# Input weights kept and reloaded by chunks of 128 columns through four slots; token chunks that hold both blocks; turned values written back into the output tile

## The chip, the cores and the metric

The kernel runs on one core of one Trainium2 chip. The metric is the device time of one execution in microseconds (us), lower is better. All data are float32.

## What is computed

One layer of an encoder trunk on x of 1024 tokens by 1024 channels: a projection of the normed input into 3592 columns, two groups of heads that mix the tokens, an output projection, and a feed-forward part that gathers expert rows.

```python
def hybrid_layer(x, ...):
    h = rms_norm(x, norm1_w)
    proj = jnp.einsum('bsd,dc->bsc', h, w_in)
    ...   # q, k, v of the attention heads; q, k, v, gate, a, b of the delta net
    o_sb = rms_norm(stick_breaking_attention(sq, sk, sv), ...)
    qkv = jax.nn.silu(causal_depthwise_conv(gdn_qkv, gdn_conv_w))
    ...
    o_gdn = rms_norm(gated_delta_net(gq, gk, gv, log_decay, write), gdn_out_norm_w) * gate
    x = x + jnp.einsum('bsc,cd->bsd', jnp.concatenate([o_sb, o_gdn], -1), w_out)
    x = x + peer_ffn(rms_norm(x, norm2_w), peer_w_q, ...)
    return x

def peer_ffn(hn, ...):   # for each token 8 heads x 16 experts out of 16384
    u = u_table[eb]                                   # 128 rows of 4 KB a token
    act = gelu(einsum('thkd,td->thk', u, xb)) * gb
    vv = v_table[eb]                                  # 128 more
    return einsum('thk,thkd->td', act, vv)
```

## The kernel before, in words

The eight blocks of 128 tokens are worked through one after the other. Two loads dominate: for each block, 128 gathers of `peer_u` rows and 128 of `peer_v` rows (512 KB each), issued by GpSimd (POOL) into `u_ring` (9 slots) and `v_ring` (8 slots). VectorE (DVE) takes a dot product with each u row tile (L1163); TensorE (PE) multiplies each v row tile with a one-column weight that ScalarE (ACT) makes (L813) and adds it up in `va`. These row tiles belong to earlier blocks than the one whose mixing runs; a table (`SHARES`, `PACE`, `table()`) says how many u and v tiles each engine has done by each of 450 named points of the program, and gives POOL its order of issue.

The input projection is done for two blocks at a time, in four segments g = 0 to 3: segment 0 ahead of all gathers, segment g ahead of block 2g. A segment has 28 chunks of 128 columns, kinds `g`, `s`, `v`, `a`, `z`, in pairs: `g` and `s` are normed, `v` (chunks 4, 5, 16, 17) is turned to have tokens on the partitions, `a` (10, 11, 22, 23) and `z` (24 to 27) have tokens on the partitions from the start. In its loop n every engine does one stage of a different chunk: PE multiplies chunk n into PSUM bank n % 2 of `zz` (for `g`, `s`, `v`: 8 matmuls of 128 columns of weights against 256 tokens; for `a`, `z`: 8 matmuls of one block's 128 tokens against the pair's 256 columns, so that chunk n holds one block), ACT copies it out, DVE does the convolution, and at n - 6 brings chunk m = n - 6 into `o_ring[m % 4]` (L1242 to L1257, L1259) after the store of chunk m - 4 has landed.

SyncE (SP) issues the transfers, in one order of its own. In loop n it stores the turned `v` chunk n - 7 (L563), for even n it loads a pair of weights (L548), then stores chunk n - 5 (L576, L580). Segment 0 loads weights from `w_in` by pairs (1 MB), four pairs ahead, and saves each pair in the scratch `d_w` (L553). Segments 1 to 3 load them from `d_w`, again 1 MB at a time, into two slots, after PE has finished the pair two before. SP waits in place for each of these, so what stands behind a waiting store is issued late.

Of the kernel before, what the change touches and what calls it, by code (L numbers as in the profile page):

```python
# [13 lines left out]
P = 128  # L14
# [14 lines left out]
EPS = 1e-6  # L29
# [8 lines left out]
SEG = 2  # L38
ST = SEG * P
NSEG = NB // SEG  # L40
# [7 lines left out]
PW = 2  # L48
# [29 lines left out]
def stored(n):  # L78
    return CH[n][0] != "v"


# [4 lines left out]
def stores_before(n, slot):  # L86
    return sum(stored(m) for m in range(slot, n, 4))
# [33 lines left out]
def segment_before(b):  # L121

    return b // SEG if b >= 2 and b % SEG == 0 else None


def token_turn_pending(n):
# [4 lines left out]
SHARES = {"start": ((6, 6, 6), (7.2, 6, 6)),  # L131
          "level": ((6, 6, 5.9, 6, 6), (6, 6, 6, 6, 8.2)),
          "state": ((7, 7), (7, 9.8)),
          "key": ((9, 9, 9), (9, 9, 9)),
          "mix": ((7.1,), (8,)),
          "out": ((10.8, 10), (7, 10)),
          "hn": ((8,), (9.3,)),
          "pq": ((10, 9.8, 10, 10), (10, 15.9, 10, 10)),
          "score": ((7.9,), (29.7,)),
          "top": ((7, 7, 7, 8.5, 7), (7, 7, 7, 11, 7)),  # L140
          "p": ((5, 7.1, 5, 2.5), (5, 5.3, 5, 2.5))}
# [3 lines left out]
def shares(name, k, count):  # L145

    u, v = SHARES[name]
    if name == "key":
        i = 0 if k == 0 else 2 if k == count - 1 else 1
    elif name == "p":  # L150
        i = 0 if k < 4 else 3 if k >= NCH else 1 if k < GV_END else 2
    else:
        i = k
    return u[i], v[i]


def points():


    for b in range(1, NB):  # L160
        if segment_before(b) is not None:
            for n in range(NCH + 9):
                yield ("p", segment_before(b), n), *shares("p", n, 0), None if n < 4 or token_turn_pending(n) else 1
        for name, count in (("start", 3), ("level", 5), ("state", 2), ("key", b + 1), ("mix", 1), ("out", 2), ("hn", 1),
                            ("pq", 4), ("score", 1), ("top", 5)):
            for k in range(count):
                yield (name, b, k), *shares(name, k, count), FREE_BANK[name]
# [7 lines left out]
def table():  # L175
# [12 lines left out]
    for b, (u1, v1) in PACE.items():  # L188
# [11 lines left out]
        i0, u0, v0 = last[b], u1, v1  # L200
    k = 0
# [41 lines left out]
def hybrid_layer_kernel(nc, x, norm1_w, w_in, sb_q_norm_w, sb_k_norm_w, sb_out_norm_w, gdn_conv_w,  # L243
# [9 lines left out]
    d_w = scratch("d_w", (NP, P, KC * 256))  # L253
# [11 lines left out]
    with ctx:  # L265
# [57 lines left out]
        class Area:  # L323
            def __init__(self, base):
# [3 lines left out]
                def tile(n):  # L328
                    return base[:, A0 + n * ST:A0 + (n + 1) * ST]

                def pairs(ap):
                    return ap.rearrange("p (b c) -> p b c", b=SEG)

                self.xT = base[:, 0:KC * ST].rearrange("p (k t) -> p k t", k=KC)
                self.w_slots = [weights(base, 2), *(weights(v_flat, n) for n in range(PW_FIRST - PW)), weights(base, 1)]

                self.x_seg = base[:, 2048:2048 + SEG * D].rearrange("p (n d) -> p n d", n=SEG)
                self.x_scratch = base[:, 0:D]
                self.s_ring = [tile(n) for n in range(6)] + [tile(20)]
                self.e_ring = [tile(6 + n) for n in range(2)]  # L340
                self.sq_ring = [tile(8 + n) for n in range(2)]
                self.y_ring = [tile(10 + n) for n in range(2)]
                self.o_ring = [tile(12 + n) for n in range(4)]
                self.tok_ring = [tile(16 + n) for n in range(2)]
                self.tmp = [tile(18), tile(19)]
                cb0 = A0 + 21 * ST
                self.cb = [base[:, cb0 + n * 264:cb0 + n * 264 + ST + 3] for n in range(2)]
                ab = cb0 + 2 * 264
                self.ab_out, self.ab_e, self.ab_y = base[:, ab:ab + 16], base[:, ab + 16:ab + 32], base[:, ab + 32:ab + 40]
                self.ab_o3, self.ab_y3, self.ab_e3 = pairs(self.ab_out), pairs(self.ab_y), pairs(self.ab_e[:, 8:16])  # L350

        areas = [Area(w_q_t)] + [Area(work)] * (NSEG - 1)
        hist = hist_t[:, :].rearrange("p (c k) -> p c k", c=12)
        mm_bank = [bank(zz, 0)[:, 0:ST], bank(zz, 1)[:, 0:ST]]
        ss_bank = [bank(rr, 0)[:, 0:ST], bank(rr, 1)[:, 0:ST], bank(ox, 0)[:, 0:ST]]
        tr_bank = bank(ox, 1)[:, 0:ST]
        ab_bank = bank(ox, 1)[:, 0:16]
        ab3 = ab_bank.rearrange("p (b c) -> p b c", b=SEG)
# [60 lines left out]
        ss8, ms8, y8, a8, r8 = (sm[:, 120 + 8 * n:120 + 8 * n + SEG] for n in range(5))  # L419
# [5 lines left out]
        x_landed = [sem(f"x_landed{n}") for n in range(SEG)]  # L425
# [13 lines left out]
        tok_stored = [sem(f"tok_stored{n}") for n in range(2)]  # L439
# [73 lines left out]
        def slot_of(g, j):  # L513

            if g == 0:
                return j % PW_FIRST, j // PW_FIRST
            slot = (0, PW_FIRST - 1)[j % PW]
            first = len(range(slot, NP, PW_FIRST))
            return slot, first + (NP // PW) * (g - 1) + j // PW

        def w_slot(g, j):
            return areas[g].w_slots[slot_of(g, j)[0]]

        @block.sync
        def _(sp):
            def x_loads(g):
                if g:
                    sp.wait_ge(h_done, SEG * g)
                for n in range(SEG):
                    sp.dma_start(areas[g].x_seg[:, n, :], x_blk[SEG * g + n]).then_inc(x_landed[n], 16)  # L530

            def w_load(g, j):
                slot, times = slot_of(g, j)
                ahead = PW_FIRST if g == 0 else PW
                if j >= ahead:
                    sp.wait_ge(projected, NCH * g + 2 * (j - ahead) + 2)
                elif j == ahead - 1:
                    sp.wait_ge(x_turned, SEG * (g + 1))
                elif g:
                    sp.wait_ge(best_shifted, SEG * g)  # L540
                if g == 0 and j >= ahead:
                    sp.wait_ge(w_saved[slot], 16 * times)
                if g == 0:
                    col = PAIR_COLS[PAIRS[j][0]] + 256 * PAIRS[j][1]
                    src = w_in[0].rearrange("(k p) n -> p k n", p=P)[:, :, col:col + 256]
                else:
                    src = d_w[j].rearrange("p (k c) -> p k c", k=KC)
                sp.dma_start(w_slot(g, j), src).then_inc(w_landed[slot], 16)  # L548

            def w_save(j):  # L550
                slot, times = slot_of(0, j)
                sp.wait_ge(w_landed[slot], 16 * (times + 1))
                sp.dma_start(d_w[j].rearrange("p (k c) -> p k c", k=KC), w_slot(0, j)).then_inc(w_saved[slot], 16)  # L553

            def projection(g):
                b0 = SEG * g
                ahead = PW_FIRST if g == 0 else PW
                for n in range(NCH + 7):
                    m = n - 7
                    if m >= 0 and needs_tokens(m):  # L560
                        t = token_count(m) - 1
                        sp.wait_ge(turned_copied, TOKS * g + t + 1)
# [1379 lines left out]
```

## Time and profile before

| | |
|---|---|
| median of 3 runs | 3694.66 us (3689.73 to 3706.08) |
| profiled execution, its own time | 3676.49 us |
| its span, first to last instruction | 3674.5 us |
| mean granted TensorE clock | 0.786 of full |
| busy: PE, DVE, POOL, ACT | 67%, 64%, 63%, 24% |

No engine is busy all the time; the 16 DMA engines of the core are, nearly, from about 370 us on. Every number below is of the profiled execution.

### The profile page before, as it was taken

How to read it: one execution, taken by the hardware profiler on the slowest of the kernel's cores; microseconds unless marked ns; L12 is line 12 of the kernel's file. 1: busy time of each engine (PE TensorE's matmuls, PEld its weight loads, DVE VectorE, ACT ScalarE, POOL GpSimd, SP SyncE). 2: the span in 40 equal slices, each digit the busy share in tenths (PEclk: the TensorE clock that was granted, in tenths of full speed). 3: DMA queues.
4: the chain of work that ended last, by engine and by line, in shares of the span. 5: the costliest groups of instructions: out<-in, count | busy, mean ns of one | idle time of the engine just before them, and what ended most of it. 6: DMA issues, size and time to landing. Idle time of an engine off the chain costs nothing.

```text
span 3674.5 us, 44635 instructions
## 1 busy us (share of the span) xinstructions
PE 2450.8 (67%) x15137; PEld 1389.0 (38%) x15137; DVE 2333.9 (64%) x5605; ACT 869.4 (24%) x2454; POOL 2303.8 (63%) x2091
## 2 busy tenths in 40 slices
PE   7686656857568587578568577578658753444466
PEld 6565524644244255343144155344234310111122
DVE  4538987866866877566866777666777575444300
ACT  4323212322113133232123133223113210111111
POOL 0004775655666777666766767666776677666665
PEclk9898777978788689788589789789778875555589
DMA  7725998999899999999999999999999999999998
GB/s 239 257 78 172 348 328 296 400 352 327 318 338 361 352 399 413 402 345 352 358 350 373 351 352 413 384 375 365 365 347 384 351 340 361 370 364 364 361 367 324
DMA packets 389011, 1258.29 MB, mean 342 GB/s; under 512 B 43630, under 2 KB 92851, under 8 KB 380595
## 3 DMA queue, kind: packets, MB, share of 16 engines
q0 software_dynamic: 294912, 1073.87, 78.1%
q1 hardware_dynamic: 75442, 139.62, 10.4%
q10 hardware_dynamic: 18432, 41.95, 3.2%
q8 instruction: 123, 2.02, 0.2%
q14 instruction: 102, 0.83, 0.1%
HBM read 1217.50 MB, written 37.78 MB: 342 GB/s over the span
## 4 chain that ended last, share of the span: by engine, by line
PE 26%; DVE 26%; issue 15%; POOL 13%; DMA 7%; another core or an unknown queue 5%; ACT 3%; DVEq 3%; ACTq 1%; SPq 0%; POOLq 0%
PE zz L1614 12%; DVE u_ring L1163 10%; PE va L1614 8%; POOL u_ring L732 7%; POOL v_ring L749 6%; DMA v_ring<-in_peer_v,idxT 3%; DMA u_ring<-in_peer_u,idx 3%; PE rr L1614 3%; PE ox L1614 2%; DVE work L1379 1%; DVE work L1220 1%; PE rr L1618 1%; DVE work L1361 1%; DVE work L1444 1%
## 5 line engine op out<-in xcount | busy, mean ns | idle before, releaser
L732 POOL DMA_INDIRECT u_ring<-in_peer_u,idx x1024 | 1193.4, 1165 | 824.0 <-issue 286.8
L749 POOL DMA_INDIRECT v_ring<-in_peer_v,idxT x960 | 1041.3, 1085 | 499.5 <-issue 252.7
L1614 PE MATMUL va<-v_ring,column 128*32 128x256 f32 x7680 | 828.0, 488 | 566.3 <-DMA v_ring<-in_peer_v,idxT 328.9
L1163 DVE SCALAR_TENSOR_TENSOR u_ring<-u_ring,hn_t 128x1024 f32<-128x1024 f32 x896 | 1058.8, 1221 | 110.9 <-DMA u_ring<-in_peer_u,idx 82.2
L1614 PE MATMUL zz<-work 128*128 128x256 f32 (+3 forms) x2880 | 667.1, 393 | 109.6 <-issue 48.8
L1614 PEld LDWEIGHTS va<-v_ring,column 128*32 128x32 f32 x7680 | 259.6, 126 | 1098.1 <-issue 520.9
L1614 PEld LDWEIGHTS zz<-work 128*128 128x128 f32 (+1 forms) x2880 | 490.7, 212 | 310.2 <-issue 194.4
L813 ACT ACTIVATE column<-onehot,wT 128x32 f32<-128x32 f32 x1024 | 277.0, 314 | 919.2 <-remote 442.8
L1163 DVE SCALAR_TENSOR_TENSOR u_ring<-u_ring,zz 128x1024 f32<-128x1024 f32 x128 | 155.6, 1220 | 193.2 <-DMA u_ring<-in_peer_u,idx 173.3
L1614 PE MATMUL rr<-work,later 128*128 128x512 f32 x144 | 101.2, 807 | 68.2 <-DVE work L1364 35.7
L1570 DVE TENSOR_TENSOR y_buf<-va,y_buf 128x1024 f32<-128x1024 f32 x8 | 9.8, 1219 | 207.4 <-PE va L1614 201.5
L1614 PE MATMUL rr<-w_q_t,work 128*128 128x512 f32 x224 | 116.7, 668 | 0.4 <-issue 0.4
L1614 PE MATMUL zz<-w_q_t,work 128*128 128x512 f32 x224 | 103.4, 603 | 2.8 <-issue 2.7
L1614 PE MATMUL ox<-work 128*128 128x64 f32 (+1 forms) x704 | 97.1, 292 | 8.6 <-ACT work L1006 5.3
L1614 PEld LDWEIGHTS ox<-work 128*128 128x128 f32 x704 | 89.8, 205 | 30.2 <-issue 30.1
L1614 PE MATMUL rr<-work 128*128 128x128 f32 x512 | 76.6, 301 | 23.0 <-issue 8.4
L1368 DVE SCALAR_TENSOR_TENSOR work<-zz,work 128x512 f32<-128x512 f32 x72 | 49.3, 685 | 65.9 <-remote 41.0
L1361 DVE SCALAR_TENSOR_TENSOR work<-zz,work 128x512 f32<-128x512 f32 x72 | 49.3, 685 | 62.0 <-ACT work L998 50.7
L1614 PEld LDWEIGHTS rr<-work 128*128 128x128 f32 x512 | 70.5, 215 | 30.3 <-issue 11.0
L1614 PE MATMUL va<-u_ring,column 128*32 128x256 f32 x512 | 66.1, 427 | 23.2 <-issue 19.7
L749 POOL DMA_INDIRECT u_ring<-in_peer_v,idxT x64 | 60.0, 937 | 32.3 <-issue 15.9
L1614 PE MATMUL rr<-work,rest 128*128 128x512 f32 x112 | 66.5, 716 | 15.9 <-DVE work L1379 8.7
(315 smaller groups left out, 2773.7 us busy)
## 6 DMA issues: line engine op xcount, KB each, us to landing
work<-d_w SPq DMA_DIRECT2D x42, 1024.0 KB
work<-in_w_out ACTq DMA_DIRECT2D x64, 512.0 KB
u_ring<-in_peer_u,idx POOLq DMA_INDIRECT x1024
v_ring<-in_peer_v,idxT POOLq DMA_INDIRECT x960
work<-d_kT SPq DMA_DIRECT2D x36, 256.0 KB
work<-d_v SPq DMA_DIRECT2D x36, 256.0 KB
w_q_t<-in_peer_w_q SPq DMA_DIRECT2D x1, 8192.0 KB, 24.1
w_q_t<-in_w_in SPq DMA_DIRECT2D x7, 1024.0 KB
```

The costliest lines, as they stand in the source:

```text
L732: g.indirect_dma_start(u_ring[:, n % RU, :], None, u_rows, bass.IndirectOffsetOnAxis(idx[b % 2][:, s:s + 1], 0)).then_inc(u_landed[n % RU] ...
L749: g.indirect_dma_start(v_row(n), None, v_rows, bass.IndirectOffsetOnAxis(idxT[b % 3][:, t:t + 1], 0)).then_inc(v_landed[slot] if slot < RV ...
L813: a.activation(column[:, m % RC, :], onehot[:, 31 - g:63 - g], ACT.Copy, scale=wT[b % 2][:, 32 * k + g:32 * k + g + 1]).then_inc(column_do ...
L1163: v.scalar_tensor_tensor(u_ring[:, m % RU, :], u_ring[:, m % RU, :], 1.0, token, ALU.mult, ALU.mult, accum_out=dots[:, s:s + 1]).then_inc( ...
L1220: last = v.scalar_tensor_tensor(areas[g].s_ring[n % 7], areas[g].cb[c % 2][:, k:k + ST], vecs[:, w[k]:w[k] + 1], areas[g].s_ring[n % 7], A ...
L1361: sp = v.scalar_tensor_tensor(att_sp[hg], bank(zz, hg), 0.0, att_l[hg], ALU.max, ALU.add)
L1368: v.scalar_tensor_tensor(att_u[hg], bank(zz, hg), 0.0, att_l[hg], ALU.min, ALU.subtract).then_inc(z_used, 1)
L1379: arg = v.tensor_tensor(att_u[hg], att_u[hg], bank(rr, hg), ALU.subtract)
L1444: v.max_index(top_i[:, h, c, 8:16], top_v[:, h, c, 8:16], sc[:, h, c, :])
L1570: v.tensor_tensor(y_buf[:, :], va[:, :], y_buf[:, :], ALU.add).then_inc(y_done, 1)
L1614: return t_.matmul(out_, lhsT, rhs, start=start, stop=stop, skip_group_check=True)
L1618: last = t_.transpose(dst[:, c * P:(c + 1) * P], src[:, c * P:(c + 1) * P], ident[:, :])
```

## The change

1. `d_w` holds 28 chunks of 128 columns in place of 14 pairs. Segment 0 still loads pairs, and saves each pair with two transfers, each from 8 pieces of 512 bytes in every partition. Segments 1 to 3 load one chunk (512 KB, 4 KB in each partition) at a time into four slots that take the place of the two, four chunks ahead.
2. Chunks of kinds `a` and `z` hold both blocks and 128 columns in place of one block and 256: 16 matmuls of 128 columns for 8 of 256. Their stores have rows of 512 bytes for rows of 1 KB.
3. The turned `v` chunk is copied back into its own tile `o_ring[m % 4]`; `tok_ring` is gone, and the tile is free for chunk m + 4 only when the store of the turned values has landed. The three steps of the norm (L1242 to L1246) write into the output tile, so DVE's wait for its store stands ahead of the first of them.
4. The sizes of the segments come from a list, `SIZES = (2, 2, 2, 2)`; the branches for a size of 3 are not used. The tables of shares are written by block, with one difference in values: in a segment, chunks 16 to 19 have 5 u shares in place of 7.1 (and 5 v shares in place of 5.3). The floors added to `table()` change nothing by themselves.

```diff
-    d_w = scratch("d_w", (NP, P, KC * 256))
+    d_w = scratch("d_w", (NCH, P, KC * P))
...
+                        self.w_slots = [chunk(n) for n in (4, 5, 2, 3)]
...
             def w_save(j):
-                slot, times = slot_of(0, j)
+                slot, times = slot_of(0, 2 * j)
                 sp.wait_ge(w_landed[slot], 16 * (times + 1))
-                sp.dma_start(d_w[j].rearrange("p (k c) -> p k c", k=KC), w_slot(0, j)).then_inc(w_saved[slot], 16)
+                for n in (2 * j, 2 * j + 1):
+                    sp.dma_start(d_w[n].rearrange("p (k c) -> p k c", k=KC), w_of(0, n)).then_inc(w_saved[slot], 16)
+
+            def w_load(g, n):
+                slot, times = slot_of(g, n)
+                if n >= ahead(g):
+                    sp.wait_ge(projected, NCH * g + n - ahead(g) + 1)
+                elif n == 2:
+                    sp.wait_ge(x_turned, FIRST_OF[g + 1])
+                elif n == 0:
+                    sp.wait_ge(best_shifted, FIRST_OF[g])
+                sp.dma_start(w_of(g, n), d_w[n].rearrange("p (k c) -> p k c", k=KC)).then_inc(w_landed[slot], 16)
...
+                    if g and n + ahead(g) < NCH:
+                        w_load(g, n + ahead(g))
...
-                        if t >= 2:
-                            act.wait_ge(tok_stored[t % 2], 16 * ((TOKS // 2) * g + t // 2))
-                        a.activation(areas[g].tok_ring[t % 2], tr_bank, ACT.Copy).then_inc(turned_copied, 1)
+                        a.activation(areas[g].o_ring[m % 4], areas[g].tr_bank, ACT.Copy).then_inc(turned_copied, 1)
...
+                        o = areas[g].o_ring[m % 4]
+                        if g or m >= 4:
+                            dve.wait_ge(o_stored[m % 4], 16 * (stores_before(NCH, m % 4) * g + stores_before(m, m % 4)))
...
-                            v.tensor_tensor(t0, y, y, ALU.mult)
+                            v.tensor_tensor(o, y, y, ALU.mult)
...
-                        for k in range(KC):
-                            if kind in "az":
-                                last = mm(mm_bank[n % 2], areas[g].xT[:, k, P * (n % 2):P * (n % 2) + P], wc[:, k, :], k == 0, k == KC - 1)
+                        if kind in "az":
+                            for p in range(SIZES[g]):
+                                for k in range(KC):
+                                    last = mm(mm_bank[n % 2][:, P * p:P * p + P], areas[g].xT[:, k, P * p:P * p + P], wc[:, k, :], k == 0,
+                                              k == KC - 1)
```

SP's order in segment 1, from the load of chunks 14 and 15 on (`d_w` is the load of weights, `d_gv` the store of a turned `v` chunk, the other `d_` names are stores of other chunks). Before:

```order
L548 DMA work<-d_w 128x2048 [waits projected]
L563 DMA d_gv<-work 128x2x128 [waits turned_copied]
L576 DMA d_gqT<-work 128x2x128 [waits normed]
L563 DMA d_gv<-work 128x2x128 [waits turned_copied]
L548 DMA work<-d_w 128x2048 [waits projected]
L576 DMA d_gqT<-work 128x2x128 [waits normed]
```

The same place now, from the loads of chunks 13 and 14 on:

```order
L602 DMA work<-d_w 128x1024 [waits projected] x2
L610 DMA d_gv<-work 128x2x128 [waits turned_copied]
L602 DMA work<-d_w 128x1024 [waits projected]
L627 DMA d_gqT<-work 128x2x128 [waits normed]
L610 DMA d_gv<-work 128x2x128 [waits turned_copied]
L602 DMA work<-d_w 128x1024 [waits projected]
L627 DMA d_gqT<-work 128x2x128 [waits normed]
L602 DMA work<-d_w 128x1024 [waits projected]
```

The load of chunk 16 keeps its place behind the two `d_gv` stores and is half as large; chunk 15, which came ahead of both with its pair, is now loaded between them, and chunk 17 a store later.

DVE in segment 1, chunk 8, whose tile held the turned chunk 4 (`u_ring,dots` are dot products; `o_stored0` counts landed stores of tile 0). Before:

```order
L1233 TENSOR_TENSOR work<-work 128x256 [waits exp_done]
L1242 TENSOR_TENSOR work<-work 128x256 [waits seeded]
L1244 SCALAR_TENSOR_TENSOR work<-rr,work 128x256
L1246 SCALAR_TENSOR_TENSOR work<-work 128x256
L1257 SCALAR_TENSOR_TENSOR work<-work,vecs 128x256 [waits turned,o_stored0]
```

Now:

```order
L1277 TENSOR_TENSOR work<-work 128x256 [waits exp_done]
L1289 TENSOR_TENSOR work<-work 128x256 [waits o_stored0,seeded]
L1291 SCALAR_TENSOR_TENSOR work<-rr,work 128x256
L1293 SCALAR_TENSOR_TENSOR work<-work 128x256
L1300 SCALAR_TENSOR_TENSOR work<-work,vecs 128x256
```

The wait has moved three operations up, and `o_stored0` now counts the store of the turned values too.

## Rows read from the trace of the kernel before

**Rows 1.** The page's head and the DMA line of its 40 slices (91.9 us each).

```profile
span 3674.5 us, 44635 instructions
...
DMA  7725998999899999999999999999999999999998
```

**Rows 2.** Stretches: busy us of each engine, granted clock, DMA share, GB/s.

```profile
0.00:160.00 160.00, 118.18 (x544) 100.96 (x545) 72.78 (x210) 63.44 (x174) 9.14 (x43) 0.95 0.70 231
600.00:790.00 190.00, 148.51 (x865) 107.14 (x857) 140.07 (x314) 63.48 (x196) 120.77 (x106) 0.90 0.98 375
1290.00:1490.00 200.00, 162.79 (x954) 111.84 (x954) 146.61 (x319) 62.07 (x199) 149.54 (x125) 0.89 1.02 407
3060.00:3400.00 340.00, 152.13 (x946) 42.99 (x946) 149.89 (x250) 35.55 (x124) 227.24 (x237) 0.55 0.98 366
```

**Rows 3.** The segments' matmuls, grouped by shape: busy, mean ns, idle before.

```profile
L1614 PE MATMUL zz<-work 128*128 128x256 f32 x1344 | 346.4, 415 | 17.7 <-issue 10.4 <-DMA work<-d_w 7.2
```

**Rows 4.** Chain that ended last, in segment 1: start us, us, what.

```profile
689.81 10.30 DMA work<-d_w
700.15 6.67 PE zz L1614 x16
...
736.65 11.04 DMA work<-d_w
747.73 3.73 PE zz L1614 x16
...
778.41 6.20 DMA d_v<-work
```

**Rows 5.** PE's timeline in segment 1: chunks 16, 24 and 27.

```profile
700.15 6.66 PE L1614 MATMUL zz<-work 128*128 128x256 f32 x16 [1.83 <-DMA work<-d_w]
...
747.73 3.72 PE L1614 MATMUL zz<-work 128*128 128x256 f32 x16 [1.77 <-DMA work<-d_w]
...
763.32 3.72 PE L1614 MATMUL zz<-work 128*128 128x256 f32 x16
```

**Rows 6.** SP's timeline in segment 1.

```profile
689.81 0.47 SPq L548 DMA_DIRECT2D work<-d_w  x1
...
736.65 0.47 SPq L548 DMA_DIRECT2D work<-d_w  x1
...
753.42 0.36 SPq L563 DMA_DIRECT2D d_gv<-work  x1
...
761.11 0.36 SPq L563 DMA_DIRECT2D d_gv<-work  x1
```

**Rows 7.** PE's timeline in segment 2: chunk 16.

```profile
1411.82 5.41 PE L1614 MATMUL zz<-work 128*128 128x256 f32 x16 [3.64 <-DMA work<-d_w]
```

**Rows 8.** SP's timeline in segment 2: the load for that chunk.

```profile
1400.23 0.47 SPq L548 DMA_DIRECT2D work<-d_w  x1
```

**Rows 9.** DVE's timeline in segment 1: first norm step of chunk 21.

```profile
770.49 0.42 DVE L1242 TENSOR_TENSOR work<-work 128x256 f32<-128x256 f32 x1
```

**Rows 10.** PE's timeline in block 0, matmuls of 128 columns back to back.

```profile
261.21 3.74 PE L1614 MATMUL zz<-work,w_q_t 128*128 128x128 f32 x32
264.78 3.74 PE L1614 MATMUL rr<-work,w_q_t 128*128 128x128 f32 x32
```

**Rows 11.** Chain that ended last, in segment 0.

```profile
124.65 3.47 PE zz L1614 x16
130.60 3.47 PE zz L1614 x16
148.60 4.76 DMA d_kT<-w_q_t
```

**Rows 12.** SP's timeline at the end of segment 0.

```profile
146.17 0.44 SPq L553 DMA_DIRECT2D d_w<-v_ring  x1
148.60 0.37 SPq L576 DMA_DIRECT2D d_kT<-w_q_t  x1
```

**Rows 13.** DMA queues from 129 to 137 us, two stores with rows of 512 bytes: packets, MB, share.

```profile
q1 hardware_dynamic: 544, 0.26, 11.5%
```

**Rows 14.** DMA queues from 160 to 182 us, one load with rows of 8 KB.

```profile
q1 hardware_dynamic: 1183, 8.64, 94.4%
```

**Rows 15.** DMA queues from 1350 to 1460 us: gathers of rows of 4 KB (q0), SP's transfers (q1).

```profile
q0 software_dynamic: 9817, 35.75, 80.3%
q1 hardware_dynamic: 5152, 9.58, 22.5%
```

More of the change, by code:

```diff
@@ L34 @@
 GELU_S = math.sqrt(2.0 / math.pi)
-SEG = 2
-ST = SEG * P
-NSEG = NB // SEG
+SIZES = (2, 2, 2, 2)
+NSEG = len(SIZES)
+FIRST_OF = [sum(SIZES[:g]) for g in range(NSEG + 1)]
 PAIR_COLS = {"g": COL_G, "v": COL_G + 8 * P, "s": 0, "a": COL_SV, "z": COL_GATE}
@@ L47 @@
 NCH = len(CH)
-PW = 2
 PW_FIRST = 4
@@ L86, in stores_before @@
 def stores_before(n, slot):
-    return sum(stored(m) for m in range(slot, n, 4))
+    return len(range(slot, n, 4))
 NORMS, CONVS, SILUS, TOKS = norm_count(NCH - 1), conv_count(NCH - 1), silu_count(NCH - 1), token_count(NCH - 1)
@@ L323, in hybrid_layer_kernel, with __init__, pairs, chunk @@
         class Area:
-            def __init__(self, base):
+            def __init__(self, g):
+                size = SIZES[g]
+                st = size * P
+                base = work if g else w_q_t
+                spare = hn_t[FIRST_OF[g] % 2]
+                def pairs(ap):
+                    return ap.rearrange("p (b c) -> p b c", b=size)
+                def chunk(n):
+                    return base[:, 1024 * n:1024 * (n + 1)].rearrange("p (k c) -> p k c", k=KC)
                 def weights(t, n):
@@ L355, in hybrid_layer_kernel @@
[L355 to L358, printed above, removed]
+                self.size, self.st, self.first = size, st, FIRST_OF[g]
+                self.xT = base[:, 0:KC * st].rearrange("p (k t) -> p k t", k=KC)
+                self.x_scratch = base[:, 0:D]
+                if size == 3:
+                    starts = [3072 + n * st for n in range(2)] + [A0 + n * st for n in range(16)]
+                    self.x_seg = [base[:, 3072:4096], base[:, 7168:8192], spare[:, :]]
+                    self.w_slots = [chunk(n) for n in (4, 5)]
+                    conv, cb0 = spare, 0
+                    o_first, others = 10, (7, 8, 9, 14, 15, 16)
+                else:
+                    starts = [A0 + n * st for n in range(17)]
+                    self.x_seg = [base[:, 2048 + n * D:2048 + (n + 1) * D] for n in range(size)]
+                    if g == 0:
+                        self.w_slots = [weights(base, 2), weights(v_flat, 0), weights(v_flat, 1), weights(base, 1)]
+                    else:
+                        self.w_slots = [chunk(n) for n in (4, 5, 2, 3)]
+                    conv, cb0 = base, A0 + 21 * st
+                    o_first, others = 12, (7, 8, 9, 10, 11, 16)
@@ L360, in hybrid_layer_kernel @@
+                self.ab_bank = bank(ox, 1)[:, 0:8 * size]
+                self.ab3 = pairs(self.ab_bank)
+                self.pairs = pairs
+        areas = [Area(g) for g in range(NSEG)]
+        hist = hist_t[:, :].rearrange("p (c k) -> p c k", c=12)
         u_flat = u_ring[:, :, :].rearrange("p s d -> p (s d)")
@@ L511, in hybrid_layer_kernel, with slot_of, w_of @@
         block = ctx.enter_context(nc.Block())
-        def slot_of(g, j):
+        def slot_of(g, n):
             if g == 0:
[L516 to L522, printed above, removed]
+                return n // 2 % PW_FIRST, n // 2 // PW_FIRST
+            slot = n % ahead(g)
+            loads = len(range(slot, NP, PW_FIRST)) + sum(len(range(slot, NCH, ahead(i))) for i in range(1, g) if slot < ahead(i))
+            return slot, loads + n // ahead(g)
+        def w_of(g, n):
+            w = areas[g].w_slots[slot_of(g, n)[0]]
+            return w if g else w[:, :, P * (n % 2):P * (n % 2) + P]
         @block.sync
@@ L527, in x_loads @@
                 if g:
[L528 to L548, printed above, removed]
+                    sp.wait_ge(h_done, FIRST_OF[g])
@@ L668, in _ @@
                     x_loads(g)
-                    for j in range(PW):
-                        w_load(g, j)
+                    for n in range(ahead(g)):
+                        w_load(g, n)
                     projection(g)
```

281 lines of the change are left out of this document (152 added, 129 removed).

## The prediction

> **What bounds the kernel now.** I read the page first. PE, DVE and POOL are each busy about two thirds of the span, but the DMA line stands at 9 in nearly every slice from the fifth on [rows 1]. By stretches, segment 2 of the projection has a DMA share of 1.02 at 407 GB/s, segment 1 has 0.98 at 375, and a late stretch of gathers alone 0.98 at 366 [rows 2]. The transfers are the floor there, and the change moves the same bytes. Segment 0 has a share of 0.70: it goes by the chain through PE, ACT and DVE. Then I looked for waits that the change can touch. Among all matmuls of segments 1 to 3 PE waited 7.2 us for weights, in three waits [rows 3]: 1.83 and 1.77 us in segment 1 [rows 5] and 3.64 us in segment 2 [rows 7]. In segment 1 both lie on the chain that ended last, behind loads of 10.30 and 11.04 us [rows 4], since SP issued them late.
>
> **The change part by part.** The sum is made against the profiled execution's own 3676.49 us, which is 18.2 us under the median of the runs, 3694.66.
>
> *Loads by chunk (takes away).* PE was ready for chunk 16 at 700.15 - 1.83 = 698.3 and for chunk 24 at 747.73 - 1.77 = 746.0 [rows 5]. Their loads were issued at 689.8 and 736.7 [rows 6], which leaves 8.5 and 9.3 us; in segment 2, 1411.82 - 3.64 - 1400.23 = 8.0 us [rows 7, 8]. SP's order keeps each of these loads at its place, with half the bytes. No row shows a 512 KB load in such a crowd. The bounds are a store of 128 KB, 6.20 us, and a load of 1 MB, 10.30 to 11.04 us [rows 4]. A straight line between 128 KB and 1 MB (10.7) gives 6.2 + 4.5 x 384/896 = 8.1 us; I take this, since it is the middle of two like cases. So all three waits go, or shrink to under 0.5 us: up to -7.2 us. Behind a wait PE's matmuls were also slower: the group of chunk 16 took 6.66 us in segment 1 and 5.41 in segment 2, against 3.72 for the usual one [rows 5, 7]. At most -7.2 - 2.9 - 1.7 = -11.8 us. But while PE waited, the DMA engines did not: the gathers went on at full share, and a PE that is earlier then waits for rows. Segment 2 (1.02) I count at nothing, and of segment 1 (1.77 + 1.83 + 2.9 = 6.5 us, at 0.98) about half: **-3**, with the ends 0 and -11.8.
>
> *New places in SP's order.* Chunk 15's load now stands behind the first `d_gv` store and chunk 27's behind the third, in place of ahead of both. For chunk 27 in segment 1: store at 753.42, load at once behind it, landed by 753.9 + 8.1 = 762.0, wanted at 763.32 [rows 5, 6]. 1.3 us to spare, the least of all; the cover is the four chunks of PE work between. If the load takes the 10.3 us of a whole pair, PE waits 0.9 us, and ACT and DVE behind it. I take **0**, with the end +0.9 x 3 segments = +2.7.
>
> *The turned values in the output tile.* DVE now waits, for chunks 8, 9, 20 and 21, until the store of the turned chunk four before has landed; queued behind that wait are this chunk's norm, the dot products of its point, and through `normed` both ACT and SP. In segment 1 the last of these stores was issued at 761.11 [rows 6] and, at 6.20 us, lands at 767.3; DVE comes to chunk 21 at 770.49 [rows 9]. 3.2 us to spare, so **0**. The wait that moves up over three operations (three times 0.42) is for a store older still. ACT loses its wait for `tok_ring`, on which no row shows idle time: nothing.
>
> *Matmuls of `a` and `z` chunks.* 16 in place of 8, in the trace two passes each: 32 passes of 128 columns start 3.57 us apart as a group [rows 10], 16 of 256 columns take 3.47 [rows 11]. +0.1 us for each of 32 chunks. The 24 in segments 1 to 3 lie under DMA time (0, at most +2.4); of the 8 in segment 0 I put half on the chain: **+0.4**.
>
> *Saves in rows of 512 bytes.* Two stores with such rows kept the engines busy 0.115 x 8 x 16 = 14.7 us for 0.26 MB, 28 ns a packet, about 285 GB/s [rows 13]; rows of 8 KB moved 8.64 MB in 0.944 x 22 = 20.8 us, 416 GB/s [rows 14]. A pair's save so goes from 2.5 to 3.7 us, +1.2. Thirteen of the 14 are covered: SP only comes later to a load that is wanted three pairs on, and to stores that DVE wants four chunks on. The last is not: it is issued at 146.17, ahead of the store of chunk 21 at 148.60 [rows 12], whose landing, 4.76 us, is on the chain [rows 11]. **+1.2**.
>
> *Other packets.* Eight stores a segment go from rows of 1 KB to 512 bytes: at most 1.05 MB at 285 instead of 407 GB/s, +1.1 us of DMA time; most of them come at the segment's end, where I count half: three times 0.5 = **+1.5**. The weights go from packets of 8 KB to 4 KB. Gathered 4 KB rows in segment 2 took 0.803 x 110 x 16 / 9817 = 144 ns for 3.64 KB on average [rows 15], 25.3 bytes a ns and engine or 405 GB/s, against 416: 14.7 MB a segment, +1 us, three times half under cover: **+1.5**. The end of this term is a rival.
>
> Sum: -3 + 0 + 0 + 0.4 + 1.2 + 1.5 + 1.5 = **+1.6 us**, 3678 for the profile. For the median I add no more than this and round: **3695 us**. What a measurement of this kernel can tell from no change is about 0.5%, 18 us.
>
> The Trainium skill speaks against this change: its page "DMA: Bandwidth & Descriptors", section Bandwidth, has the rule to batch transfers to 1 MiB or more. Its fit of 2.0 us plus bytes at 436 GB/s would make a load 4.4 us as a pair and 3.2 us as a chunk, so 42 x 4.4 = 185 us against 84 x 3.2 = 269 us if they ran one at a time. As an estimate from that page this is +84 us, but four of them can be in flight, and the trace's own 10 us for a loaded pair says that the crowd, not the fixed part, sets the time.
>
> **Rivals.**
>
> *A, the relief passes through.* The three waits and the slow groups behind them go in full, -11.8; and the order of the gathers, of which 506 of 2048 stand one or two places elsewhere, falls well: two dot products (1.2 us each) for each of three segments, -7.3. With the costs of 4.6 us above taken as covered, 3694.7 - 11.8 - 7.3 = 3676. For: both loads are on the chain of segment 1. Against: a share of 0.98 to 1.02. Chance 0.18.
>
> *B, smaller packets cost the DMA engines their rate (slower).* The place is segments 1 to 3, the price 44 MB of weights. If packets of 4 KB from SP's queue move as a gather alone does, 366 GB/s [rows 2], and not at 416: 120.3 - 105.9 = +14.4 us. With the full 3.3 us for stores, 2.4 for matmuls and 1.6 in segment 0, and without the relief: 3694.7 + 14.4 + 3.3 + 2.4 + 1.6 = 3716. For: the gathers' 366. Against: 405 in segment 2, where the gathers' rows of 4 KB share the engines with the second queue. It decides from a rate of about 375 on. Chance 0.14.
>
> By the same page of the Trainium skill, section "Queues, rings and completion order", an engine takes turns between its queues packet by packet, which would leave SP's loads a smaller share of the turn when their rows are half as long. No row here separates the two queues' turns.
>
> *C, a new wait.* The turned store takes over 9.4 us instead of 6.2 (3.2 spare), or the chunk load over 9.4 (1.3 spare), in each segment. The price is what is over, some 1 to 2 us, four times a segment in three segments: up to +12: 3694.7 + 12 = 3707. That is inside 0.5%. Chance 0.10.
>
> **How the numbers follow.** Forecast as such, within some 8 us: 0.58; A 0.18; B 0.14; C 0.10. Within 0.5% (3676 to 3713) lie the forecast, C and a part of A and B (some 0.02 each); the rest of A is faster, of B slower. The gathers' order can push either way by its 7 us, which moves 0.01 or so more to each side. That makes faster 0.17, same 0.69, slower 0.14. The range of eight in ten goes from A's 3676 less some of the runs' own spread (5 us below the median before) to B's end: 3674 to 3716.
>
> **What would show it.** Right: the matmuls `zz<-work` of 256 columns wait under 1 us for weights; SP's 84 loads land in 7 to 9 us; DMA share and GB/s of the segments as before; the store of chunk 21 in segment 0 lands 1 us later, and block 0 starts 1 to 2 us later. Wrong: segment 1 shorter by over 8 us with block 3 starting earlier (A); segments at 375 to 390 GB/s with a share of 1.0 (B); DVE idle before its first norm step with a `d_gv` store named, or PE idle before chunk 27 (C). What would upset the whole is a shift of gathers against consumers in the long stretches between the segments, which hold most of the time and which no row of mine prices beyond single rows.

## The result

| | before | changed |
|---|---|---|
| median of 12 runs each | 3691.47 us | 3727.77 us |
| ratio, 95% interval | | 1.0088 (1.0063 to 1.0113) |
| profiled execution, own time | 3676.49 us | 3742.13 us |
| span, mean granted clock | 3674.5 us, 0.786 | 3740.3 us, 0.782 |

The change made the kernel slower: by 0.88% as a ratio, some 32 us; the two medians differ by 36.3 us. The forecast was no change, 3695 us, with a range that ended at 3716.

The page's head and DMA line of the changed kernel answer to [rows 1]:

```profile
span 3740.3 us, 45675 instructions
...
DMA  8725997998999999999999999899999999999999
```

Windows over the three segments, from the gates of the block ahead to the first copy of the block behind. First before, then changed (busy us of PE, PEld, DVE, ACT, POOL, granted clock, DMA share, GB/s):

```profile
604.70:795.20 190.50, 144.89 (x808) 105.55 (x808) 135.74 (x307) 61.35 (x186) 120.97 (x107) 0.88 0.98 377
1299.70:1527.00 227.30, 172.32 (x1018) 117.14 (x1018) 160.23 (x349) 67.72 (x215) 169.75 (x142) 0.85 1.02 404
2138.70:2369.10 230.40, 170.06 (x1006) 115.92 (x1002) 161.95 (x353) 67.51 (x214) 163.67 (x142) 0.87 1.02 397
```

```profile
607.60:810.80 203.20, 150.75 (x957) 113.40 (x949) 134.01 (x304) 61.35 (x186) 114.71 (x100) 0.86 0.91 337
1329.60:1565.10 235.50, 174.99 (x1137) 120.41 (x1137) 157.32 (x346) 67.50 (x215) 159.14 (x136) 0.87 0.99 375
2177.00:2429.60 252.60, 180.54 (x1138) 125.67 (x1138) 159.06 (x349) 67.52 (x214) 154.55 (x136) 0.82 0.94 353
```

The segments are 12.7, 8.2 and 22.2 us longer, and their DMA engines are less busy, not more. This suggests that something ahead of the transfers has become slower. DVE and POOL have even less to do in them. Blocks 0 and 1, behind segment 0, start only 0.7 and 0.8 us late (first copies at 155.2 and 324.1 us, for 154.5 and 323.3).

These are one profile of each kernel, and a stretch varies from profile to profile. The time from the copy of chunk 0 to that of chunk 27 of segment 1 is 147.6 us before and 160.6 us in the changed kernel, but 146.5 to 159.0 us in the profiles of the kernels below that keep the old use of u. So no single one of the three differences is a price.

The matmuls of the segments now stand in two shapes; this is the row of the larger one in the changed kernel, and it answers to [rows 3]. PE's waits of [rows 3] for loads of weights are gone from it. In the whole trace one wait of 2.1 us is left, of PE's weight load (PEld), in segment 2:

```profile
L1657 PE MATMUL zz<-work 128*128 128x256 f32 x960 | 257.0, 422 | 26.0 <-issue 25.0 <-ACT idxT L1128 0.9
```

An `a` or `z` chunk takes 3.84 us, against 3.72 in [rows 5] (PE's timeline in segment 1):

```profile
753.01 3.84 PE L1657 MATMUL zz<-work 128*128 128x128 f32 x32
```

### The profile page after: what moved, and what is told of

Same layout as the page of the kernel before. It is cut to its first block, busy times and chain, and to the rows that moved or that the text cites. A ratio compares the mean times of both kernels' runs of the same rounds, so it can differ in the third digit from the quotient of the medians.

```text
span 3740.3 us, 45675 instructions
## 1 busy us (share of the span) xinstructions
PE 2481.4 (66%) x15649; PEld 1423.9 (38%) x15649; DVE 2333.9 (62%) x5605; ACT 869.0 (23%) x2454; POOL 2307.6 (62%) x2091
## 4 chain that ended last, share of the span: by engine, by line
DVE 26%; PE 25%; issue 15%; POOL 14%; another core or an unknown queue 7%; DMA 6%; ACT 4%; DVEq 3%; ACTq 1%; SPq 0%; POOLq 0%
PE zz L1657 12%; DVE u_ring L1203 10%; POOL u_ring L774 8%; PE va L1657 7%; POOL v_ring L791 6%; DMA u_ring<-in_peer_u,idx 3%; PE rr L1657 3%; DMA v_ring<-in_peer_v,idxT 2%; PE ox L1657 2%; DVE work L1264 1%; DVE work L1542 1%; DVE work L1544 1%; DVE work L1487 1%; DVE work L1422 1%
## 5 line engine op out<-in xcount | busy, mean ns | idle before, releaser
L1657 PE MATMUL va<-v_ring,column 128*32 128x256 f32 x7680 | 837.1, 489 | 563.7 <-DMA v_ring<-in_peer_v,idxT 305.0
L1657 PE MATMUL zz<-work 128*128 128x128 f32 (+3 forms) x3264 | 675.9, 368 | 117.4 <-issue 63.5
L1657 PEld LDWEIGHTS zz<-work 128*128 128x128 f32 (+1 forms) x3264 | 510.6, 212 | 313.6 <-issue 216.5
L1657 PE MATMUL ox<-work 128*128 128x64 f32 (+1 forms) x704 | 97.8, 293 | 14.7 <-ACT work L1046 11.7
L1661 PE MATMUL ox<-ident,work 128*128 128x128 f32 x88 | 21.2, 373 | 83.3 <-DVE work L1361 53.5
```

Source lines behind the costliest of these rows:

```text
L1657: return t_.matmul(out_, lhsT, rhs, start=start, stop=stop, skip_group_check=True)
```

## The experiments

Every ratio is to the kernel before, run on the same chip in the same rounds, with its 95% interval.

### One part of the change undone at a time

The loss shows from chunk 2 of a segment on and most around chunks 11 to 13, which fitted several of the edits. So four kernels each undid one of them in the changed kernel.

*The table of shares:*

```diff
-            "p": ((5, 7.1, 7.1, 7.1, 5, 5, 5, 2.5, 2.5, 2.5),)}
+            "p": ((5, 7.1, 7.1, 7.1, 7.1, 5, 5, 2.5, 2.5, 2.5),)}
...
-            "p": ((5, 5.3, 5.3, 5.3, 5, 5, 5, 2.5, 2.5, 2.5),)}
+            "p": ((5, 5.3, 5.3, 5.3, 5.3, 5, 5, 2.5, 2.5, 2.5),)}
```

> The changed kernel with one thing undone: chunks 16 to 19 of a segment have 7.1 u shares and 5.3 v shares again, in place of 5 and 5. The order of the gathers and all times at which the engines take dot products and rows are those of before. Theory S (the table): the two blocks' worth of dot products moved out of chunks 16 to 19 to the later chunks make the segments longer, since the loss of 32 us stands in and right around them. Then this kernel is at about 3691 us, ratio to before 0.998 to 1.003, and segment 1 lasts 191 us again (203 now). Theory O (one of the other edits: loads, a and z chunks, output tile): no change against the changed kernel, ratio 1.006 to 1.012, segment 1 still over 200 us.

*The turned values in tiles of their own:*

```diff
-                        a.activation(areas[g].o_ring[m % 4], areas[g].tr_bank, ACT.Copy).then_inc(turned_copied, 1)
+                        if t >= 2:
+                            act.wait_ge(tok_stored[t % 2], 16 * ((TOKS // 2) * g + t // 2))
+                        a.activation(areas[g].tok_ring[t % 2], areas[g].tr_bank, ACT.Copy).then_inc(turned_copied, 1)
```

> The changed kernel with the turned values in two tiles of their own again, and the norm's steps in two tiles of their own, so that DVE's wait for the store stands ahead of its last step only and does not count the turned store. Theory T (the tile): DVE waits for the turned stores in the crowd, where I had 3.2 us to spare; the segments lose most around chunks 8 to 13 and 20 to 25, as the traces show. Then most of the 36 us come back: ratio 0.998 to 1.003. The rivals: ratio 1.006 to 1.012, and DVE's idle time before the norm's steps is under 3 us in all.

*Weights by pairs:*

```diff
-                        self.w_slots = [chunk(n) for n in (4, 5, 2, 3)]
+                        self.w_slots = [weights(base, 2), weights(base, 1)]
...
             def w_load(g, n):
+                if n % 2:
+                    return
                 slot, times = slot_of(g, n)
                 if n >= ahead(g):
-                    sp.wait_ge(projected, NCH * g + n - ahead(g) + 1)
+                    sp.wait_ge(projected, NCH * g + n - ahead(g) + 2)
```

> The changed kernel with weights by pairs again: d_w of 14 pairs, one save with rows of 8 KB, in segments 1 to 3 one load of 1 MB for two chunks into two slots. Chunks a and z still hold both blocks. Theory B (small packets and more loads cost the rate, or SP's many waits in place): the three segments come back by 8 to 20 us each, ratio 0.998 to 1.003. The rivals: ratio 1.006 to 1.012; the waits for weights come back (4 to 10 us in all), and that is all that can be seen.

*Chunks `a` and `z` with one block each:*

```diff
-                            for p in range(SIZES[g]):
-                                for k in range(KC):
-                                    last = mm(mm_bank[n % 2][:, P * p:P * p + P], areas[g].xT[:, k, P * p:P * p + P], wc[:, k, :], k == 0,
-                                              k == KC - 1)
+                            for k in range(KC):
+                                last = mm(mm_bank[n % 2], areas[g].xT[:, k, P * (n % 2):P * (n % 2) + P], w2(k), k == 0, k == KC - 1)
```

> The changed kernel with the a and z chunks of before: one block and 256 columns, 8 matmuls of 256 columns, whose weights lie in two of the four slots; the load into the first of these waits until both have been read. Theory M (twice as many PE instructions, 128 more passes a segment, and stores in rows of 512 bytes, at chunks 10, 11, 22 to 27): the loss stands right behind these chunks, and comes back: ratio 0.998 to 1.003. The rivals: ratio 1.005 to 1.012.

| kernel | ratio |
|---|---|
| old shares | 1.0034 (1.0004 to 1.0064) |
| turned values in their own tiles | 1.0085 (1.0056 to 1.0115) |
| weights by pairs | 1.0105 (1.0072 to 1.0137) |
| `a`, `z` by block | 1.0105 (1.0061 to 1.0149) |

With the old shares segment 1 lasts 186.7 us for 203.2, as Theory S wanted, and the ratio ends just above its bound of 1.003. Only the table gives time back, about 0.54 of the 0.88%. Two numbers in a table, which I had counted at nothing, outweigh all the transfers and matmuls that I had worked out. The other three edits, undone, give nothing that can be told from the changed kernel.

### The table alone, and what else is left

```diff
-        i = 0 if k < 4 else 3 if k >= NCH else 1 if k < GV_END else 2
+        i = 0 if k < 4 else 3 if k >= NCH else 1 if k < 16 else 2
```

> The kernel before with only the table of the change: chunks 16 to 19 of a segment at 5 u and 5 v shares. Theory S (the table is most of the loss, as its undoing gave back 0.54%): ratio to before 1.004 to 1.008. Rival I (the table costs only together with the other edits, for example because the a chunks and the turned tiles have moved the crowd): ratio 0.998 to 1.002.

Three more kernels have the old shares and one other part undone, with the edits shown above.

> The changed kernel with the old shares and the turned values in tiles of their own: what is left of the loss, 0.34%, if the output tile's waits make it. Theory T2: ratio 0.998 to 1.001. Otherwise 1.002 to 1.006.

> The changed kernel with the old shares and weights by pairs. If packets and SP's added waits make the 0.34% that is left (my rival B in small): 0.998 to 1.001. If loads by chunk are worth the 3 us of my sum or nothing: 1.003 to 1.006.

> The changed kernel with the old shares and a and z chunks of one block and 256 columns. If their matmuls and stores in rows of 512 bytes (2.4 + 3.3 + 1 us at the upper ends of my terms) make what is left: 0.999 to 1.002. If not: 1.002 to 1.006.

The table alone gave **1.0070 (1.0041 to 1.0100)**: it needs none of the other edits. Of the rest, tiles gave 1.0045 (1.0012 to 1.0078), pairs 1.0012 (0.9984 to 1.0041), `a` and `z` by block 1.0025 (0.9992 to 1.0058), against 1.0034 for the old shares alone. The intervals overlap, so none of the three is shown to make the rest; with pairs it is smallest, between the two ranges that I had written down for it.

### Shares of u or of v; the order of issue or the points of use

The table sets two things: POOL's order of issue, of which 506 of 2048 entries differ, and the points at which DVE takes dot products (134 of 450 counts differ, all but one of them by one or two) and PE takes rows of v (25 differ, by one). A kernel can take one from the one table and one from the other:

```diff
+RAISED[0] = 16
+_, OTHER_U, OTHER_V, *_ = table()
+ORDER = list(issue_order(OTHER_U, OTHER_V))
```

> The kernel before with the u shares of the change alone (5 for 7.1 in chunks 16 to 19; the v shares stay at 5.3). Theory D (dot products that DVE takes out of chunks 16 to 19, where the chain has room, and into chunks 5 to 15 and the block behind the segment, where it has none): the whole price of the table, ratio 1.004 to 1.008, and in segment 1 chunks 4 to 10 last 33.4 us for 32.2, one dot product of 1.2 us more. Rival V (the rows of v): 0.999 to 1.002.

> The kernel before with the v shares of the change alone (5 for 5.3 in chunks 16 to 19): 25 of 450 counts are one lower, and 82 gathers change their kind. Theory D: 0.998 to 1.002. Rival V: over 1.003.

> The kernel before, in which only POOL's order of issue comes from the table of the change; DVE, PE and ACT use the tiles at the points of before. Theory G (the gathers come in another order than the tiles are wanted, and it is their order among u and v that costs): over 1.003 here. Theory D: 0.998 to 1.003, as the engines' own work stands where it stood; a gather out of place by one or two costs at most its own 1.3 us where a consumer waits.

> The reverse: DVE, PE and ACT use the tiles at the points of the change's table, and POOL issues in the order of before. Theory D: 1.003 to 1.008, and segment 1's chunks 4 to 10 last 33.4 us. Theory G: near 1.000 if the order makes it, or above the 1.007 of the whole table if it is the mismatch between order and use that costs.

| of the change's table | ratio |
|---|---|
| u shares only | 1.0058 (1.0034 to 1.0083) |
| v shares only | 1.0030 (1.0000 to 1.0060) |
| POOL's order only | 0.9974 (0.9945 to 1.0003) |
| points of use only | 1.0082 (1.0049 to 1.0115) |

Theory G falls: the order costs nothing, and gathers out of step with their use cost nothing that shows (1.0082 for the points of use alone, 1.0070 for the whole table). The points of use carry the whole price, most of it by u. The v alone missed Theory D's bound of 1.002, but its interval reaches 1.000.

Why a dot product costs there, a window over chunks 4 to 10 of segment 1 shows (copy of chunk 4 to copy of chunk 10). Before, all engines:

```profile
638.00:670.20 32.20, 27.82 (x161) 20.09 (x159) 29.40 (x71) 13.77 (x42) 19.41 (x18) 1.00 0.98 376
```

and the dot products' line of it alone, DVE busy (two records for one dot product; the window's edges cut through some):

```profile
638.00:670.20 32.20, 12.04 (x21) 1.00 0.98 376
```

The same two of the changed kernel:

```profile
648.20:681.60 33.40, 28.20 (x178) 21.00 (x176) 30.60 (x73) 13.77 (x41) 20.60 (x18) 1.00 0.96 344
```

```profile
648.20:681.60 33.40, 13.00 (x22) 1.00 0.96 344
```

DVE is busy 29.40 of 32.20 us, then 30.60 of 33.40: it sets the pace, with gaps of some tenths between its operations. One dot product more, and the stretch is 1.2 us longer. It was 32.2 or 32.3 us in every kernel with the old use of u or the late half alone, and 33.3 or 33.4 in every one that puts one dot product more there (the change's table, its early half, and the two kernels with 9.2 shares further on), whatever its loads, tiles or chunks. Here Theory D's number came out as written. The chain that ended last, there, in the kernel before, goes through DVE piece after piece:

```profile
640.77 2.29 DVE u_ring L1163 x4
643.82 0.48 DVE work L1220
...
652.60 0.42 DVE work L1257
653.02 1.14 DVEq L1215
654.16 1.15 DVE u_ring L1163 x3
```

This 1.2 us alone is not the price. At chunk 11 of segment 1 the counts of both tables are equal again, so the dot product is only taken earlier, and the time is lost right behind. From the copy of chunk 10 to that of chunk 12 of segment 1, in the kernel before and in the one with the early half (all engines):

```profile
670.20:680.00 9.80, 9.80 (x56) 7.51 (x56) 8.53 (x16) 2.61 (x9) 7.70 (x6) 1.00 1.02 399
```

```profile
673.00:686.60 13.60, 11.71 (x56) 8.21 (x56) 7.40 (x14) 2.62 (x9) 10.70 (x10) 0.88 1.01 408
```

DVE has one dot product less there and PE the same matmuls, and still the stretch takes 13.6 us for 9.8. It is 13.5 to 13.7 us in all four kernels that add the table's early u to the kernel before (u shares, points of use, early half, whole table), and 16.5 in the changed kernel, but 10.7 in the changed kernel with `a` and `z` by block. The two kernels with 9.2 shares also have 33.3 or 33.4 us in chunks 4 to 10, but their dot product comes from ahead of chunk 4, their next stretch takes 9.8 us, and they were not slower. What makes the 3.8 us is not settled.

### Early half and late half

In the change's table 16 counts are higher by one, in chunks 5 to 15, and 118 lower, all but one by one or two, from chunk 16 on and through most of the block behind. The larger, or the smaller, of the two tables' counts makes each half alone (`max` in the first kernel):

```diff
+        u = [min(a, c) for a, c in zip(u, other[0])]
+        v = [min(a, c) for a, c in zip(v, other[1])]
```

> The kernel before, with the larger of the two tables' counts at each point of use (POOL's order of before): the 16 places in chunks 5 to 15 at which the change's table has one dot product more, and no more. Theory D1 (one dot product early in chunks 5 to 15 is what costs): 1.003 to 1.008. Theory D2 (the dot products that come one or two late, behind chunk 16 and into the next block): 0.999 to 1.002, though segment 1's chunks 4 to 10 last 33.4 us for 32.2.

> The kernel before, with the smaller of the two tables' counts at each point of use (POOL's order of before): the 118 places from chunk 16 on and in the block behind at which one or two dot products are done later, and block 4's weights one chunk later. Theory D2: 1.003 to 1.008, with the first half of blocks 2, 4 and 6 longer by 4 to 10 us. Theory D1: 0.999 to 1.002.

The early half gave **1.0041 (1.0014 to 1.0068)**, the late half **1.0102 (1.0065 to 1.0139)**. Both cost, so neither D1 nor D2 alone holds; the late half is the larger. Together they would make 1.43%, where both at once measured 0.82% (1.0082, 1.0049 to 1.0115): their sizes do not simply add up, and the late half rests on 6 runs. Its cost shows in the block behind the segment. First half of block 2, from its first copy to the end of its mixing, before and with the late half (all engines):

```profile
795.20:894.90 99.70, 72.80 (x516) 48.33 (x516) 72.89 (x135) 28.14 (x64) 54.31 (x47) 0.83 0.88 319
```

```profile
791.20:897.20 106.00, 76.97 (x516) 51.16 (x516) 75.75 (x140) 28.25 (x64) 60.42 (x54) 0.81 0.91 334
```

DVE does 30 dot products in it for 28, the two that the segment has passed on: 2.9 us more of its time, 6.3 us more on the clock. In block 6, before and with the late half:

```profile
2369.10:2532.60 163.50, 125.20 (x900) 74.78 (x900) 113.90 (x204) 54.28 (x124) 109.81 (x99) 0.87 0.98 376
```

```profile
2360.40:2537.00 176.60, 132.42 (x900) 80.42 (x900) 115.35 (x206) 54.12 (x124) 118.15 (x107) 0.79 0.98 371
```

One dot product more is 1.5 us; the stretch is 13.1 us longer. The same 900 matmul records take 7.2 us more, at a granted clock of 0.79 for 0.87 of the 2.4 GHz level.

All profiles together, 11 with the old or an earlier use of u against 9 with the late one: block 2's half lasts 101.7 us on average against 105.5, block 6's 165.3 against 173.7. The second spreads widely (154.9 to 175.2, and 162.3 to 179.9), so the 13.1 us of the pair above are in part the luck of two profiles.

### Block 4's weights

> The late half of the table's use again (smaller counts from chunk 16 on, POOL's order of before), but with the one count kept that holds block 4's weights at chunk 18 of segment 3. Theory D2 (each late dot product costs, wherever it falls): about as the late half, 1.006 to 1.013, and the stretch from chunk 27 of segment 3 to the end of block 6's mixing over 198 us, as with all late kernels (188 to 195 otherwise). Theory W (the weights of block 4 one chunk later cost, since ScalarE and TensorE turn them and all its rows wait for that): 1.000 to 1.004.

```diff
+        i = names.index(("p", 3, 18))
+        u[i] = other[0][i]
```

**1.0071 (1.0043 to 1.0100)**, for 1.0102 with that count lowered too. The late dot products cost by themselves; whether the weights' place adds to it, the intervals do not tell. Block 6's half was short here, against what I had expected:

```profile
2373.70:2536.00 162.30, 120.42 (x900) 71.98 (x900) 115.78 (x205) 53.92 (x124) 120.03 (x105) 0.88 1.01 389
```

The dot product is there (115.78 of DVE), but the clock is 0.88. So a late dot product does not by itself make this stretch 13 us longer: in these two profiles the difference goes with the clock. Whether block 4's weights have a part in it, one profile of each does not tell.

### The other way, and a faster version

9.2 u shares in chunks 16 to 19 for 7.1:

```diff
-          "p": ((5, 7.1, 5, 2.5), (5, 5.3, 5, 2.5))}
+          "p": ((5, 7.1, 9.2, 5, 2.5), (5, 5.3, 5.3, 5, 2.5))}
```

> The kernel before with the step made the other way: chunks 16 to 19 at 9.2 u shares for 7.1, so that one or two dot products are done earlier from chunk 16 on. Theory D as a slope (the more work in chunks 16 to 19, the better): 0.993 to 0.998. Theory D as an optimum near the old value (the old table was tuned, either side costs): 1.001 to 1.006.

The same points of use, with POOL's order from the change's table:

```diff
+LATE[0] = 3
+_, OTHER_U, OTHER_V, *_ = table()
+ORDER = list(issue_order(OTHER_U, OTHER_V))
```

> A version meant to be faster than both: the kernel before with 9.2 u shares in chunks 16 to 19 at the points of use, and POOL's order of the change's table. If the two effects seen singly (0.9974 for the order, 0.9986 for the use) are real and add up: 0.993 to 0.997. If both were chance, or the gathers of u now come too late for the earlier use: 0.999 to 1.004.

0.9986 (0.9962 to 1.0011) and 1.0004 (0.9977 to 1.0030). The first lies between the ranges of its two theories. More use earlier gains nothing that can be measured, and no version beat the kernel before. The slope ends about at the old value.

### Loads by chunk alone

The kernel before with only its loads and saves changed, as in the change's diff. PE starts an `a` or `z` chunk there only when both chunks of its pair have landed, since it still takes 256 columns.

> The kernel before with loads by chunk alone: 84 loads of 512 KB through four slots and saves in rows of 512 bytes; shares, a and z chunks and the turned values' tiles as before. My sum for this part is -3 + 1.2 + 1.5 = 0: 0.998 to 1.002. Rival B in small (packets and SP's added waits make what is left of the loss): 1.002 to 1.005. Rival A (the waits for weights go and the gain passes through): 0.995 to 0.998.

**1.0017 (0.9995 to 1.0040)**, as forecast. But PE's waits for weights did not go. Waits of PE in this kernel, and in the changed kernel with the old shares:

```profile
PE zz L1680 <- DMA work<-d_w: 4.5, 3, 3.5
```

```profile
PE zz L1657 <- DMA work<-d_w: 3.5, 3, 3.0
```

and the loads on the chain that ended last, in the same two kernels:

```profile
692.39 11.02 DMA work<-d_w
```

```profile
693.21 9.65 DMA work<-d_w
738.00 9.82 DMA work<-d_w
```

A load of half the bytes took 9.65, 9.82 and 11.02 us, against 10.30 and 11.04 for a whole pair in [rows 4]. A landing can be read only where an engine waited for it, so these are loads that came late; how long all 84 took (my sign was 7 to 9 us) the trace does not tell.

## Why the prediction was wrong

**What bounds the kernel: wrong for the segments' middle.** I wrote of the segments that "the transfers are the floor there", from a DMA share averaged over 200 us. In chunks 4 to 10 of segment 1 DVE is busy 29.4 of 32.2 us and each dot product counts in full, beside a DMA share of 0.98. The experiments confirm it: 1.2 us for one dot product, in every kernel with one more there. The 3.8 us lost in the two chunks behind it have no such account.

**The step that failed** is the one that priced the table. It stands in rival A, as "the order of the gathers, of which 506 of 2048 stand one or two places elsewhere", worth 7.3 us, and as 0.01 of chance to either side. I took the edit for an edit of POOL's order. That order costs nothing (0.9974); the points of use, which I did not price, cost 0.82%. Its two parts: one dot product early in chunks 5 to 15 (1.0041), one or two late from chunk 16 on (1.0102). I named what would upset the whole, "a shift of gathers against consumers", and had it half right: what costs is where the consumers' work stands among the engines' own, and moving the gathers along with it does not help (1.0070). For the early part a stretch shows this; for the late part it is a reading of the ratios.

**Loads by chunk, -3: not earned.** In the changed kernel the three waits were gone, as forecast, but no time was won. With the old shares, waits of 3.5 us are back, so that they were gone was in part luck. The straight line through 128 KB and 1 MB, which gave 8.1 us for a load, was the wrong way to fill the gap: the 512 KB loads on the chain measured 9.65 to 11.02 us, as those of 1 MB did. The part as a whole (-3, +1.2, +1.5) measured 1.0017 (0.9995 to 1.0040), which leaves room for my zero.

**Matmuls of `a` and `z`, +0.1 each: right** (3.84 for 3.72 us). **Saves in short rows, +1.2: not shown.** Block 0 starts 0.7 us later in the changed kernel's profile, but over the 11 profiles with segment 0 as before it starts anywhere from 153.9 to 160.5 us. **Turned values in the output tile, 0: right**; DVE's list of waits in the changed kernel has no store of a turned chunk in it, and undoing the edit gave 1.0085 for 1.0088.

**Rival B, small packets, fell.** The changed kernel did show what I had named as its sign, 375 GB/s at 0.99 in segment 2, but with shares of 0.91 and 0.94 in the other segments. With pairs again, the same stretch of segment 1 has 0.93 and the ratio stays at 1.0105. A low rate at a share under 1.0 fits gathers that were asked for late, and not slow packets. As the cause of the 0.34% that the table leaves, small packets are not excluded: old shares with pairs measured 1.0012 (0.9984 to 1.0041). By the Trainium skill's page "DMA: Bandwidth & Descriptors", section Bandwidth, transfers are to be batched to 1 MiB; no run here shows a gain from it that is clear of noise. The same page's fit of a fixed 2 us and a rate (section Anatomy of one DMA, for transfers that GpSimd issues) is far under the 10 us or so that loads of either size on the chain took in this crowd. **Rival C, a new wait, fell** too: neither a turned store nor chunk 27's load is waited for. **Rival A**'s relief did not come.

**Sums.** Rival C's price, 1 to 2 us four times in each of three segments, is +12 to +24 us and not "up to +12", so it reached beyond 0.5%. A median of 3694.66 and +1.6 make 3696, not 3695, and 14.7 us over 544 packets are 27 ns each, not 28. None of these has to do with the miss.

**What stays open.** Without the table the changed kernel is still at 1.0034 (1.0004 to 1.0064), some 12 us where my sum had 1.6. Loads by chunk alone give 1.0017; of the rest no single edit could be told from nothing. Why an early dot product costs 3.8 us in the two chunks behind it is open as well. And that the late use of one or two dot products makes a stretch longer by more than DVE's own 1.5 to 2.9 us is seen, but its reason is not settled: PE's granted clock is lower in the longer stretches, but whether it falls because PE waits for DVE, or both follow from something else, no run here tells.

## What to carry to other kernels

A table that sets where one engine's side work stands in another chain is part of the critical path, even where its edits look like leftovers: price it by the engine that does the side work, in each stretch, and not by the transfers that feed it. Before calling DMA the floor of a stretch, look at windows of 30 us instead of 200, and ask whether some engine's chain has next to no gap in it. Where a diff restructures code and changes two numbers on the way, run the two numbers alone first.

## What the runs showed of the hardware

A load of 512 KB issued in the crowd of gathers, on the chain, landed after 9.65 to 11.02 us, hardly sooner than one of 1 MB (10.30 and 11.04 us). These are three loads and two, all of them waited for.

The same 900 matmul records in block 6's first half took 119.6 to 132.5 us over the 20 profiles, at granted clocks of 0.89 to 0.79 of 2.4 GHz. The stretch was mostly longer where the clock was lower, though not always (154.9 us at 0.86 with the old shares, 177.7 at 0.82 with the table alone): 158.5 us at 0.89 with POOL's order only, 175.2 us at 0.79 in the version meant to be faster:

```profile
2380.70:2539.20 158.50, 119.63 (x900) 73.06 (x900) 113.96 (x204) 53.65 (x124) 109.58 (x97) 0.89 1.01 389
```

```profile
2358.60:2533.80 175.20, 132.54 (x900) 80.83 (x900) 114.34 (x203) 53.93 (x124) 107.12 (x97) 0.79 0.94 352
```

The two kernels differ only in where dot products are used, and their DVE time is the same to 0.4 us. PE also stalls with no wait that the profile shows. In segment 2 of the changed kernel the 32 passes of chunk 23, 3.84 us elsewhere, are strewn over 8 us, with ScalarE and DVE idle behind them (PE's timeline, its matmuls for that chunk's bank, gaps in brackets):

```profile
1503.13 1.31 PE L1657 MATMUL zz<-work 128*128 128x128 f32 x7 [0.26 <-issue]
...
1505.32 1.08 PE L1657 MATMUL zz<-work 128*128 128x128 f32 x3 [0.44 <-issue]
...
1506.75 1.21 PE L1657 MATMUL zz<-work 128*128 128x128 f32 x4 [0.35 <-issue]
```

What holds them up the trace does not show. The kernel before has such gaps too, in another place (0.35 to 1.12 us between matmuls from 2322.92 to 2326.44), so they are no part of the cause that I can show.

The spread that goes with the clock, some 17 us in one stretch, is about as large as what the whole change did in a segment, so a single profile of each kernel could not have found the cause; the ratios over many runs did.
